# A weight split announced in two halves, and TensorE starting a weight unit on its first four blocks

## The reference, cut to what matters

```
h = rmsnorm(x)                       # 520 x 1024
proj = h @ w_in                      # 1024 x 10752: q, k, v, g_ret, x_lru, y_lru, g_a, g_b
o = retention(rope(q), rope(k), v)   # 4 heads, chunked, with a state of 256 x 512 per head
ret = (silu(g_ret) * groupnorm(o)) @ w_ret_out
hl = rg_lru(causal_conv(x_lru))      # two block-diagonal gates, then a scan over time
lru = (gelu(y_lru) * hl) @ w_lru_out
x = x + (sigmoid(g_a) * ret + sigmoid(g_b) * lru) @ w_o
x = x + (silu(h2 @ w_gate) * (h2 @ w_up)) @ w_down        # h2 = rmsnorm(x), 1024 -> 2816 -> 1024
```

## Time and profile before

| | us |
|---|---|
| median of 3 runs | 2568.41 |
| the profiled execution, its own time | 2568.21 |
| its span | 2566.4 |
| TensorE busy (matmul) | 2462.4 (96%) |
| GpSimd busy | 1710.7 (67%) |
| VectorE busy | 1207.4 (47%) |
| ScalarE busy | 607.5 (24%) |

### The profile page before, as it was taken

How to read it: one execution, slowest core, us unless ns; L and a number is a source line. 1 busy time by engine, 2 the same in 40 slices (tenths; PEclk the granted TensorE clock), 3 DMA queues, 4 the chain that set the end, 5 groups by cost and what they waited for, 6 DMA issues and landing times.

```text
span 2566.4 us, 52772 instructions
## 1 busy us (share of the span) xinstructions
PE 2462.4 (96%) x19604; PEld 2385.8 (93%) x19604; DVE 1207.4 (47%) x1613; ACT 607.5 (24%) x869; POOL 1710.7 (67%) x1993
## 2 busy tenths in 40 slices
PE   7999999999989999999989999999999899999997
PEld 7899999999989999999988999999999899999997
DVE  6555555577463532022356454545863645221223
ACT  2312121325361211011113122221353612100111
POOL 5465746577776777677754656565777777776774
PEclk9999999999999999999999999999999999999998
DMA  4444545322224222222235536452222422222222
GB/s 159 171 152 167 176 162 178 135 85 83 85 79 83 97 90 83 90 94 87 90 123 193 187 134 210 137 180 103 87 82 85 78 92 91 90 82 92 96 82 84
DMA packets 120224, 298.61 MB, mean 116 GB/s; under 512 B 19136, under 2 KB 19648, under 8 KB 120064
## 3 DMA queue, kind: packets, MB, share of 16 engines
q1 hardware_dynamic: 60480, 199.78, 24.4%
q10 hardware_dynamic: 59584, 96.56, 11.3%
HBM read 255.92 MB, written 40.38 MB: 115 GB/s over the span
## 4 chain that ended last, share of the span: by engine, by line
PE 73%; POOL 7%; issue 4%; DVE 4%; DMA 4%; POOLq 3%; ACT 2%; DVEq 1%; ACTq 1%; SPq 0%
PE banks L362 67%; POOL w_low L349 7%; POOLq L346 3%; DMA w_raw<-in_wstream 3%; PE banks L536 2%; PE banks L498 1%; DVE scratch L881 1%; PE banks L552 1%; PE banks L528 1%; DMA scratch<-in_sret 1%; PE banks L515 1%; DVE rinv L700 0%; ACT scratch L1309 0%; DVE scratch L983 0%; PE banks L455 0%
## 5 line engine op out<-in xcount | busy, mean ns | idle before, releaser
L349 POOL TENSOR_TENSOR w_low<-w_raw,w_high 128x256 fp32r<-128x256 f32 (+1 forms) x1568 | 1276.7, 845 | 62.2 <-issue 3.0
L345 POOL TENSOR_SCALAR w_high<-w_raw 128x1024 fp32r<-128x1024 f32 (+3 forms) x420 | 433.6, 1032 | 770.0 <-PE banks L362 740.3
L362 PE MATMUL banks<-x_high,w_high 128*128 128x260 f32 x4096 | 843.3, 287 | 65.1 <-POOL w_low L349 36.1
L362 PE MATMUL banks<-x_high,w_low 128*128 128x260 f32 x4096 | 829.6, 284 | 0.0
L362 PE MATMUL banks<-x_low,w_high 128*128 128x260 f32 x4096 | 827.7, 284 | 0.0
L362 PEld LDWEIGHTS banks<-x_high,w_high 128*128 128x128 f32 x4096 | 635.2, 190 | 87.4 <-issue 35.1
L362 PE MATMUL banks<-split_scratch,w_high 128*128 128x260 f32 x4000 | 650.5, 285 | 10.9 <-POOL w_low L349 5.1
L362 PEld LDWEIGHTS banks<-x_high,w_low 128*128 128x128 f32 x4096 | 635.7, 190 | 0.0
L362 PEld LDWEIGHTS banks<-x_low,w_high 128*128 128x128 f32 x4096 | 635.6, 190 | 0.0
L362 PEld LDWEIGHTS banks<-split_scratch,w_high 128*128 128x128 f32 x4000 | 550.6, 189 | 21.0 <-issue 11.1
L362 PE MATMUL banks<-split_scratch,w_low 128*128 128x260 f32 x2000 | 403.9, 283 | 0.0
(11 more groups left out here) (157 smaller groups left out, 1824.7 us busy)
## 6 DMA issues: line engine op xcount, KB each, us to landing
w_raw<-in_wstream SPq DMA_DIRECT2D x268, 512.0 KB, 3.4
scratch<-in_sret ACTq DMA_DIRECT2D x64, 512.0 KB, 6.8
out_ret_s<-scratch ACTq DMA_DIRECT2D x64, 512.0 KB, 3.3
w_raw<-in_wstream SPq DMA_DIRECT2D x64, 384.0 KB, 3.0
w_raw<-in_wstream SPq DMA_DIRECT2D x40, 448.0 KB, 3.2
scratch<-v_rows ACTq DMA_DIRECT2D x64, 256.0 KB, 4.0
w_raw<-in_wstream SPq DMA_DIRECT2D x48, 320.0 KB, 2.8
out_ret_p<-scratch ACTq DMA_DIRECT2D x8, 512.0 KB, 2.8
```

Source lines behind the costliest of these rows:

```text
L345: pool.tensor_scalar(WH[:, j, w], WR[:, j, w], 1.0, 0.0, ALU.mult, ALU.add)
L349: m = pool.tensor_tensor(WL[:, j, p], WR[:, j, p], WH[:, j, p].bitcast(F32), ALU.subtract)
L362: m = pe.matmul(out, wt[:, w, blk * P:(blk + 1) * P], x[xi], start=first and n == 0, stop=last and n == 2)
```

## The change

`w_split` and `w_used` now count halves of a unit, two steps for each. `HB` is 4 blocks. GpSimd still writes the whole high part in one instruction and the low part in the same pieces, but the piece that ends block 4 raises `w_split` as well as the last one. TensorE waits for `w_split` inside `product`, at block 0 for the first half and at block 4 for the second, and its first matmul of each half raises `w_used`. GpSimd's condition for starting unit u is worked out to the same event as before, the first matmul of unit u-1 (`u2 + 3`); its two waits have changed places. SyncE's condition for loading unit u is still the whole split of unit u-2. All bases of the two counts are doubled.

```diff
+HB = 4
+assert all(HB < n <= 2 * HB for _, blocks in RUNS for n in blocks)
...
-                            sp.wait_ge(s["w_split"], layer * UNITS + (u + 1) + i * len(blocks))
+                            sp.wait_ge(s["w_split"], layer * (2 * UNITS) + 2 * (u + 1) + i * (2 * len(blocks)))
...
-            pool.sem_inc(s["w_split"], 2)
+            pool.sem_inc(s["w_split"], 4)
...
-                            u = layer * UNITS + base + k + i * len(blocks)
-                            pool.wait_ge(s["w_used"], u + 2)
+                            j = (base + k) % 2
+                            u2 = layer * (2 * UNITS) + 2 * (base + k) + i * (2 * len(blocks))
                             pool.wait_ge(w_ld[j], (layer * (UNITS // 2) + i * (len(blocks) // 2)) * 16
                                          + 16 * ((base + k) // 2 + 1))
+
+                            pool.wait_ge(s["w_used"], u2 + 3)
                             pool.sem_inc(s["go_pool"], 1)
+                            w = slice(0, n * P)
                             pool.tensor_scalar(WH[:, j, w], WR[:, j, w], 1.0, 0.0, ALU.mult, ALU.add)
                             pool.drain()
-                            for b in range(0, n, PIECE):
-                                p = slice(b * P, min(b + PIECE, n) * P)
-                                m = pool.tensor_tensor(WL[:, j, p], WR[:, j, p], WH[:, j, p].bitcast(F32),
-                                                       ALU.subtract)
-                            m.then_inc(s["w_split"], 1)
+                            for b0, b1 in ((0, HB), (HB, n)):
+                                for b in range(b0, b1, PIECE):
+                                    p = slice(b * P, min(b + PIECE, b1) * P)
+                                    m = pool.tensor_tensor(WL[:, j, p], WR[:, j, p], WH[:, j, p].bitcast(F32),
+                                                           ALU.subtract)
+                                m.then_inc(s["w_split"], 1)
...
-            def product(outs, w, blk, xs, first, last):
-                started = blk
+            def product(outs, ub, u, blk, xs, first, last):
+                w, started = u % 2, blk % HB
+                if not started:
+                    pe.wait_ge(s["w_split"], ub + (2 * u + 5 + blk // HB))
...
-            def unit_begin(ub, u):
-                pe.wait_ge(s["w_split"], ub + (u + 3))
...
-            pe.sem_inc(s["w_used"], 2)
+            pe.sem_inc(s["w_used"], 4)
...
-                            pe.wait_ge(s["w_split"], ub0 + (u + 3) + 4 * i)
```

More of the change, by code:

```diff
@@ L338, in _ @@
                         for k, n in enumerate(blocks):
-                            j, w = (base + k) % 2, slice(0, n * P)
-                            u = layer * UNITS + base + k + i * len(blocks)
-                            pool.wait_ge(s["w_used"], u + 2)
+                            j = (base + k) % 2
+                            u2 = layer * (2 * UNITS) + 2 * (base + k) + i * (2 * len(blocks))
                             pool.wait_ge(w_ld[j], (layer * (UNITS // 2) + i * (len(blocks) // 2)) * 16
                                          + 16 * ((base + k) // 2 + 1))
+                            pool.wait_ge(s["w_used"], u2 + 3)
                             pool.sem_inc(s["go_pool"], 1)
+                            w = slice(0, n * P)
                             pool.tensor_scalar(WH[:, j, w], WR[:, j, w], 1.0, 0.0, ALU.mult, ALU.add)
                             pool.drain()
-                            for b in range(0, n, PIECE):
-                                p = slice(b * P, min(b + PIECE, n) * P)
-                                m = pool.tensor_tensor(WL[:, j, p], WR[:, j, p], WH[:, j, p].bitcast(F32),
-                                                       ALU.subtract)
-                            m.then_inc(s["w_split"], 1)
+                            for b0, b1 in ((0, HB), (HB, n)):
[4 more added lines that the diff above has]
+                                m.then_inc(s["w_split"], 1)
         @block.tensor
         def _(pe):
-            def product(outs, w, blk, xs, first, last):
-                started = blk
+            def product(outs, ub, u, blk, xs, first, last):
+                w, started = u % 2, blk % HB
+                if not started:
+                    pe.wait_ge(s["w_split"], ub + (2 * u + 5 + blk // HB))
                 for n, (wt, xi) in enumerate(((WH, 0), (WH, 1), (WL, 0))):
@@ L383, in whole @@
             def whole(ub, u, tb, idx, hi, lo, made=None, count=0):
-                unit_begin(ub, u)
                 tile_begin(tb, idx)
@@ L389, in whole @@
                         pe.wait_ge(made, count + (k + 1))
-                    m = product(outs, u % 2, k, pairs(hi, lo, k), k == 0, k == MT - 1)
+                    m = product(outs, ub, u, k, pairs(hi, lo, k), k == 0, k == MT - 1)
                 m.then_inc(s["p_done"], 1)
@@ L398, in spread @@
                 for k in ks:
-                    if q % size == 0:
-                        unit_begin(ub, u + q // size)
-                    m = product(outs, (u + q // size) % 2, q % size, pairs(hi, lo, k),
+                    m = product(outs, ub, u + q // size, q % size, pairs(hi, lo, k),
                                 k == ks[0], k == ks[-1])
@@ L419, in _ @@
             with pe.Fori(0, DEPTH) as layer:
-                ub0, tb0 = layer * UNITS, layer * TILES + TILE0
+                ub0, tb0 = layer * (2 * UNITS), layer * TILES + TILE0
                 def ret_out(hh, ub, u0, tb, i0):
                     for m_ in range(MT):
-                        if m_ % 2 == 0:
-                            unit_begin(ub, u0 + m_ // 2)
                         tile_begin(tb, i0 + m_)
@@ L432, in ret_out @@
                                 pe.wait_ge(s["og_low"], hh * VT + (k + 1 - VT))
-                            m = product(outs, (u0 + m_ // 2) % 2, (m_ % 2) * VT + k, pairs(OGH, OGL, k),
+                            m = product(outs, ub, u0 + m_ // 2, (m_ % 2) * VT + k, pairs(OGH, OGL, k),
                                         k == 0, k == VT - 1)
@@ L463, in one_head @@
                     else:
-                        ub, tb = ub0 - MT // 2 + head * U_HEAD, tb0 - MT + head * T_HEAD
+                        ub, tb = ub0 - MT + head * (2 * U_HEAD), tb0 - MT + head * T_HEAD
                         ug, g0 = QK + VT + MT // 2, QK + VT + MT
@@ L610, in lru_out @@
                     for k in range(GT):
-                        m = product(outs, u % 2, k, pairs(GLH, GLL, k), k == 0, k == GT - 1)
+                        m = product(outs, ub, u, k, pairs(GLH, GLL, k), k == 0, k == GT - 1)
                     m.then_inc(s["p_done"], 1)
@@ L635, in _ @@
                     for j in range(2):
-                        place = (ub0 + 4 * i, B_MERGE + 2 * j, MERGE[0], tb0 + 4 * i)
+                        place = (ub0 + 8 * i, B_MERGE + 2 * j, MERGE[0], tb0 + 4 * i)
                         q = spread(*place, C_MERGE + 2 * j, XH, XL, range(MT), 0)
@@ L645, in _ @@
                     for j in range(2):
-                        whole(ub0 + 2 * i, B_WO + j, tb0 + 2 * i, C_WO + j, MH, ML)
+                        whole(ub0 + 4 * i, B_WO + j, tb0 + 2 * i, C_WO + j, MH, ML)
                 for f in range(FH):
@@ L656, in _ @@
                         for j in range(2):
-                            whole(ub0 + 2 * i, bu + j, tb0 + 2 * i, bt + j, XH, XL)
+                            whole(ub0 + 4 * i, bu + j, tb0 + 2 * i, bt + j, XH, XL)
                     def down(i, j, meet=False):
@@ L669, in down @@
                                     pe.wait_ge(s["f_low"], layer * (FH * FT) + (f * FT + k + 1))
-                                m = product(outs, u % 2, b, pairs(AH, AL, k), k == 0, k == FT - 1)
+                                m = product(outs, ub0 + 8 * i, u, b, pairs(AH, AL, k), k == 0, k == FT - 1)
                                 k += 1
```

## The result

The changed kernel took 2511.15 us (median of 4 runs, 2508.98 to 2512.63) beside 2567.91 us for the kernel before. The ratio is 0.9776, with a 95% interval of 0.9761 to 0.979: 57 us faster, where 45 were forecast (2523 us). The time lies inside the range given (2508 to 2550), near its low end. The profiled execution took 2510.63 us, with a span of 2508.8 us against 2566.4 before.

The account below looks back on a forecast made before the run. Matmuls bound the kernel, so only TensorE's stops could be won: 23.5 us in layer 0, 47.0 in both, added waits free, clock costing 2. 2568.2 - 47 + 2 = 2523 us, range 2508 to 2550.

Parts of the forecast that it names:

- What bounds the kernel: Whole span: matmuls bound it, TensorE busy 96%; only its stops can be won, chiefly 64 waits for GpSimd's low part, 41.1 us.
- The sum for the heads and the LRU branch, with 0.27 us for each wait: Layer 0 heads and 500 to 717 us: waits vanish, each costing 0.27 us beyond idle; 5.7 and 10.5 us kept.
- The cut at the end of the LRU branch: 717 to 767 us: of 6.6 us only 1.1 kept; 5.5 move into TensorE's wait for VectorE, growing to some 8.
- The down loops: Down tiles, seven in each of two halves: 8.22 us falls to 7.92 each, 4.2 us kept a layer.
- Added waits and raises cost nothing: 420 mid-unit waits and 420 more raises on matmuls: zero cost taken, since met waits showed none.
- rival 3: At block 4 of 420 units each met wait costs 0.27 us: 2636 us; sign, 5.76 us gate/up period lengthens; chance 0.04.
- The second half is never late: At block 4: the second half has 2.88 us, needs some 2.3 when disturbed; at most 0.3 us late, zero taken.
- The new order of GpSimd's waits: GpSimd's swapped waits and additional raise lie under its idle 770 us, so no gain or cost was counted.
- the merge and the clock: Merge: the long load's stop shrinks by 0.7 us; clock: 1 us lost a layer, 3 us either way for the range.
- ScalarE and VectorE take more of the gain: Heads and 500 to 717 us: their chains take back all gain there, 15 us remain, 2553 us; chance 0.09.
- A stop at block 4: TensorE's stop moves to block 4 because the second half is late: nothing won, 2568 us; chance 0.03.
- That TensorE is held by something else at the same moments: TensorE's unit start is held by something else, such as `t_free`, so little comes: 2560 us; chance 0.04.

## Why the prediction came out as it did

**What bounds the kernel: right.** The starts behind GpSimd's split were the winnable time. Without the early start 57 of the 64 stay, and the ratio is 0.9933.

**The sum for the heads and the LRU branch, with 0.27 us for each wait: right.** 16.2 us were forecast to unit 102 and 16.3 gained in layer 0. Layer 1 gained 18.5 us there, 1.6 of it by the clock (below). With the idle column alone the sum would have been 10 us (3.3 and 7.2, less 0.5).

**The cut at the end of the LRU branch: right.** 1.1 us forecast, 1.1 gained, the pause for VectorE at 7.8 us where 8 was said. The run with whole units there shows that the gain moves into this pause.

**The down loops: right.** One round of them in the changed kernel, TensorE's first pairs of two tiles:

```profile
1007.86 0.65 PE L369 MATMUL banks<-split_scratch,w_high 128*128 128x260 f32 x4
...
1015.78 0.65 PE L369 MATMUL banks<-split_scratch,w_high 128*128 128x260 f32 x4
```

7.92 us a tile, as forecast, where it was 8.22. The 0.30 us a tile that no wait row had shown were real: the two halves won 3.3 and 2.3 us a layer.

**Added waits and raises cost nothing: right,** for 420 of each and for 2208 more waits. The sign named for rival 3 stayed away too: a gate or up unit takes 5.77 us in both traces.

**The second half is never late: right.** No row of TensorE shows a wait for the split at block 4. Of the three waits left, two are those at the long loads of the merge, 0.62 us in layer 0 and 0.92 in layer 1. The third is the first unit of layer 1, where 2.2 us stood before:

```profile
1252.57 2.79 POOL L355 TENSOR_TENSOR w_low<-w_raw,w_high 128x256 fp32r<-128x256 f32 x4 [0.16 <-issue]
...
1255.79 0.50 PE L369 MATMUL banks<-x_high,w_high 128*128 128x260 f32 x2 [2.11 <-POOL w_low L355]
```

TensorE needs only the first two of these four pieces of 0.7 us, and they ended at 1253.99, 1.8 us before it started. So this isn't a wait for GpSimd, though the row puts it down to it, and the sign named ahead (those left stand at the two long loads) came as said. What TensorE waited for there stays open. The 41.1 us before held 2.2 us of it, which the prediction counted among layer 1's 32 waits; taking layer 1 as layer 0, it gave them no gain, rightly.

**The new order of GpSimd's waits "lies under its idle 770 us": true in the changed kernel, wrong as a reason.** The idle time is an average. Alone, the swap wins 14 us, because at the units for which TensorE waits GpSimd isn't idle: its hand-over stands in TensorE's path. It makes no difference that the runs can tell here only because the early start takes the hand-over off this path.

**The two terms that were mis-sized: the merge and the clock.** The forecast was 45 us and the two spans differ by 57.6. Some 5.5 us of what was missed lie in the merge without the clock, and some 6 in the clock, where 2 us of loss were taken and some 4 won. Units 110 to 127 were priced at 0.7 us and gained 4.2 us in layer 0 and 3.9 in layer 1, clock included. It came in three parts.
- The stop at the long load was to shrink by 0.7 us. It shrank by 1.5 us, from 2.1 (the longest of the earlier trace rows) to the 0.62 us of the next row, since the load too took 9.3 us where it had taken 10.51; in layer 1 by 2.2 us, from 3.1 (the longest of the earlier trace rows) to 0.9.

```profile
765.45 0.50 PE L369 MATMUL banks<-x_high,w_high 128*128 128x260 f32 x2 [0.62 <-POOL w_low L355]
```

- The clock around it. Stretches of the changed kernel (us, busy us and count of PE, PEld, DVE, ACT, POOL, then PEclk, DMA share, GB/s), behind the load's stop and behind the long pause, in layer 0 and in layer 1:

```profile
765.00:768.00 3.00, 2.55 (x21) 2.55 (x22) 0.70 (x1) 0.69 (x1) 2.85 (x5) 1.00 0.24 63
748.00:754.00 6.00, 5.79 (x31) 5.80 (x32) 2.44 (x4) 1.59 (x3) 3.60 (x4) 0.60 0.18 17
1984.00:1990.00 6.00, 4.87 (x28) 4.87 (x29) 3.19 (x5) 2.11 (x3) 3.61 (x4) 0.64 0.04 10
```

After the shorter stop the granted clock is 1.00, the 2.4 GHz level, where it had been 0.56, mostly 1.2 GHz, for 3 us. Unit 113 took 1.55 us less for it, and its fellow in layer 1 1.52. In no profiled execution with a stop of 0.4 to 0.9 us there is the clock low behind it. The long pause went the other way: the unit behind it took 0.5 us more in layer 0 and 1.4 in layer 1. The kernel before had these stretches behind its pause of 2.6 us, again in layer 0 and in layer 1:

```profile
766.00:772.00 6.00, 5.17 (x30) 5.18 (x31) 3.81 (x4) 1.87 (x3) 3.66 (x4) 0.72 0.27 83
2032.00:2040.00 8.00, 7.03 (x58) 7.03 (x59) 4.52 (x5) 2.30 (x5) 4.76 (x6) 1.00 0.41 76
```

The prediction had both signs in hand, a longer slow stretch after the 8 us pause and a spared one here, and took 1 us of loss a layer. The loss behind the pause is about that; the spared stretch, which the prediction named but left out of its sum, was worth 1.5 us a layer.
- Stops without an idle row. Before, a unit of the merge began like this:

```profile
800.52 0.51 PE L362 MATMUL banks<-x_high,w_high 128*128 128x260 f32 x2
800.87 0.40 PE L362 MATMUL banks<-x_low,w_high 128*128 128x260 f32 x2
```

The pair before it is at 800.25, so the steps are 0.27 and 0.35 us where 0.24 is usual: 0.14 us lost with no idle time printed. The same place after:

```profile
779.16 0.39 PE L369 MATMUL banks<-x_high,w_high 128*128 128x260 f32 x2
779.39 0.40 PE L369 MATMUL banks<-x_low,w_high 128*128 128x260 f32 x2
```

There are five such starts a layer, at every second unit from 116 to 124. With some 0.03 us at each unit between, they make about 0.8 of the 1.5 us there. The other 0.7 lie at the first w_o unit, which was priced at nothing because its last block seemed tied to VectorE. But the chain of VectorE and ScalarE to that block got 0.7 us shorter itself, and one instruction of VectorE has all of it: it takes 0.85 us in the row of the changed kernel and took 1.57 before.

```profile
826.93 0.85 DVE L1163 TENSOR_TENSOR scratch<-scratch 128x520 f32<-128x520 f32 x1 [0.21 <-issue]
```

Before, it ran beside GpSimd's high part for nearly all of that instruction's 1.06 us; now only for its last 0.3 us. This would explain why the chain did not hold the gain back; it wasn't tested by itself.

**The clock elsewhere, and luck.** The 1.2 us up to unit 10 of layer 0, forecast as nothing, are the clock too. The stretch from 34 to 38 us in the kernel before, then in the changed kernel, then in the run with a wait at every block:

```profile
34.00:38.00 4.00, 4.00 (x22) 4.00 (x22) 3.81 (x6) 0.85 (x1) 3.48 (x4) 0.57 0.42 167
...
34.00:38.00 4.00, 3.62 (x30) 3.63 (x31) 3.81 (x6) 0.26 (x1) 2.90 (x3) 1.00 0.56 221
...
34.00:38.00 4.00, 3.90 (x21) 3.91 (x22) 3.81 (x6) 0.55 (x1) 3.17 (x4) 0.61 0.54 215
```

Unit 2 took 7.39 us at the lower clock and 5.82 without it. The run with a wait at every block, as fast as the changed kernel, has the low clock back, so the change doesn't decide it. A unit of layer 1 (the 15th) is the same: 7.74 us before, 6.18 in the changed kernel, 7.7 in its second profiled execution. So of the 57 us some 4 are the clock's, an estimate by the lengths of these units and those of the merge, and 3 of them, at these two units, are luck of the profiled execution. No reading of the kernel before could have told these 3.

**Left open.** Why the load of the earlier trace rows got 1.2 us shorter isn't known; the runs show only that with the small stores moved it takes 3 us.

The rivals: that ScalarE and VectorE take more of the gain is out (only the 5 us a layer already counted). A stop at block 4 is out by the wait rows, and a price for each wait by the run with 2208 more of them. That TensorE is held by something else at the same moments is out by the whole of the gain.

## What to carry to other kernels

Where two engines hand each other buffers, count the loop of hand-overs, not their average load: GpSimd was idle for 770 us, and waiting for it still cost TensorE some 50 us. Announcing a product in parts cost nothing that these runs can tell where the waits are met, and it took the hand-over off the path nearly everywhere. A gain ahead of a pause that another chain sets goes into that pause, and a pause that is then shortened uncovers the next late thing, here a load behind small stores.

## What the runs showed of the hardware beyond what was expected

- The order of two waits ahead of an instruction matters: with the wait that ends last put last, GpSimd began 0.48 us after the start of TensorE's first matmul and not 0.61 (medians of some 410 units), worth 14 us of 2565 in the kernel before.
- A matmul that waits only briefly shows no idle time although the pace breaks: 0.14 us a start in the merge and 0.30 us a down tile, next to 0.27 us on top of each idle time that is printed.
- Beside three small stores of 135 KB together, which took 8 to 11 us to land, one weight load of 384 KB took 9.3 us in the changed kernel and one of 448 KB 8.3 us with the gate tiles read early; with the stores moved away such loads took about 3.
- After a pause of 2.1 us the granted clock was 0.56 over 3 us in the kernel before; after one of 0.62 us it was 1.00, and after one of 7.8 us 0.60 over 6 us. The spared stretch was worth 1.5 us a layer, a third of what the merge won. The length of the pause alone doesn't settle it: in the kernel before, the same pause of 2.6 us was followed by 0.72 over 6 us in layer 0 and by 1.00 over 8 us in layer 1.
